# Operands at other places in SBUF, a decay by one product, and VectorE steps in another order, in a decoder layer in split fp32

## The reference

```python
x = x + 0.5 * swiglu_ffn(x, ffn1_norm, ...)          # silu(h @ w_gate) * (h @ w_up)) @ w_down, width 2816
h = rms_norm(x, mix_norm); P = h @ w_in              # split into q,k,v,z,a,b | q,k,v | q
y = concat(gated_deltanet(...), moba_attention(...), memory_attention(...))
x = x + y @ w_out
x = x + 0.5 * swiglu_ffn(x, ffn2_norm, ...)
```

## Time and profile before

| | us |
|---|---|
| median of the runs | 994.51 |
| the profiled execution | 994.35 |
| its span | 992.5 |
| TensorE busy | 987.5 (99%) |
| VectorE busy | 685.7 (69%) |
| GpSimd busy | 509.7 (51%) |
| ScalarE busy | 444.7 (45%) |

### The profile page before, as it was taken

One profiled execution on the slowest core, in us unless ns is written; L12 is line 12 of the kernel. 1 busy time (PEld: TensorE's weight loads), 2 busy tenths in 40 slices (PEclk: granted clock), 3 DMA queues, 4 the chain that ended last, 5 costly groups with the idle time before them and its releaser, 6 DMA issues.

```text
span 992.5 us, 16521 instructions
## 1 busy us (share of the span) xinstructions
PE 987.5 (99%) x6833; PEld 872.2 (88%) x6833; DVE 685.7 (69%) x1092; ACT 444.7 (45%) x655; POOL 509.7 (51%) x297
## 2 busy tenths in 40 slices
PE   9999999999999999999999999999999999999998
PEld 7888999999999988788877888888999999999997
DVE  6894976676666497863547764789986676666745
ACT  8642444344443472534456764634343334433341
POOL 0355775676656433543252301645975666756741
PEclk9999999999999999999999999999999999999999
DMA  8432322332123312321221001322132333123312
GB/s 312 154 130 79 128 86 86 128 128 97 74 86 127 114 57 86 127 86 43 85 87 44 3 2 44 127 85 86 50 122 85 128 128 118 53 86 127 128 43 85
DMA packets 15914, 95.33 MB, mean 96 GB/s; under 512 B 2016, under 2 KB 2400, under 8 KB 5600
## 3 DMA queue, kind: packets, MB, share of 16 engines
q1 hardware_dynamic: 15696, 94.23, 26.4%
q10 hardware_dynamic: 144, 0.05, 0.0%
HBM read 92.17 MB, written 2.10 MB: 95 GB/s over the span
## 4 chain that ended last, share of the span: by engine, by line
PE 96%; DVE 3%; POOL 1%; issue 0%; ACT 0%; DVEq 0%; POOLq 0%
PE bank L2016 50%; PE bank L2142 35%; PE bank L2456 1%; PE bank L2542 1%; PE bank L2460 1%; PE bank L2482 1%; PE bank L2570 1%; PE bank L2559 1%; PE bank L2504 1%; PE bank L2194 1%; POOL wlo L517 0%; PE bank L2526 0%; DVE t_ffn_sum L1339 0%; PE bank L2606 0%; PE bank L2516 0%; PE bank L2628 0%
## 5 line engine op out<-in xcount | busy, mean ns | idle before, releaser
L2142 PE MATMUL bank<-t_ffn_hi,whi 128*128 128x256 f32 x952 | 269.4, 283 | 0.0
L2142 PE MATMUL bank<-t_ffn_hi,wlo 128*128 128x256 f32 x952 | 269.4, 283 | 0.0
L2142 PE MATMUL bank<-t_ffn_lo,whi 128*128 128x256 f32 x952 | 269.4, 283 | 0.0
L534 POOL TENSOR_TENSOR wlo<-sums,whi 128x512 fp32r<-128x512 f32 x136 | 184.7, 1380 | 131.8 <-ACT whi L739 131.7
L517 POOL TENSOR_TENSOR wlo<-raw,whi 128x1024 fp32r<-128x1024 f32 (+1 forms) x36 | 124.6, 3478 | 166.2 <-ACT whi L614 151.3
L534 POOL TENSOR_TENSOR wlo<-raw,whi 128x512 fp32r<-128x512 f32 x102 | 168.4, 1665 | 41.0 <-ACT whi L739 41.0
L2142 PEld LDWEIGHTS bank<-t_ffn_hi,whi 128*128 128x128 f32 x952 | 182.7, 192 | 0.7
L2142 PEld LDWEIGHTS bank<-t_ffn_lo,whi 128*128 128x128 f32 x952 | 182.7, 192 | 0.7
L2142 PEld LDWEIGHTS bank<-t_ffn_hi,wlo 128*128 128x128 f32 x952 | 182.7, 192 | 0.0
L2016 PE MATMUL bank<-ahi,whi 128*128 128x512 f32 x396 | 156.5, 395 | 0.4 <-POOL wlo L517 0.4
L2016 PE MATMUL bank<-ahi,wlo 128*128 128x512 f32 x396 | 154.4, 390 | 0.0
(11 more groups left out here) (339 smaller groups left out, 1405.1 us busy)
## 6 DMA issues: line engine op xcount, KB each, us to landing
raw<-fast_in SPq DMA_DIRECT2D x34, 1024.0 KB, 4.9
raw<-stream SPq DMA_DIRECT2D x26, 1024.0 KB, 4.9
raw_down<-fast_in SPq DMA_DIRECT2D x19, 1024.0 KB, 7.0
raw<-stream SPq DMA_DIRECT2D x7, 512.0 KB, 7.9
out<-x SPq DMA_DIRECT2D x7, 256.0 KB, 2.0
x<-x_in SPq DMA_DIRECT2D x3, 512.0 KB, 8.7
memx<-mem_in SPq DMA_DIRECT2D x2, 512.0 KB, 11.1
raw_gate<-stream SPq DMA_DIRECT2D x1, 1024.0 KB, 5.0
```

The costliest lines, as they stand in the source:

```text
L534: nc.gpsimd.tensor_tensor(in_ring(wlo, ring_at, n), whole[:, PIECE * at:PIECE * (at + 1)], in_ring(whi, ring_at, n).bitcast(F32), ALU.subt ...
L2142: ins = E.matmul(psum[bank][:, HALF * h:HALF * (h + 1)], a, b[:, k, :], start=start and k == 0 and m == 0, stop=k == K2 - 1 and m == 2, sk ...
```

## The change

The code below is the change without lines that only follow from it. It has four parts.

- Places. 64 bytes are left free behind `alo` and again behind `mv`, the x-sum operands get offsets. Worked out modulo 256 from the sizes: raw, whi, wlo, ck, cv, kt and what follows begin at 64; x, ahi, alo, z, mq, cq, the hidden parts stay at 0. The seven operands of the first feed-forward begin at 32. Those of the second begin at 32 (T_B11), 64 (T_1), 192 (T_3), 160 (T_2), 224 (T_B21), 64 (T_B22) and 128 (T_4), which is -96 to +192 bytes from before.
- Decay. `blocks` holds the decay in partitions 64 to 95 and the key factors in 0 to 63, so one tile serves both; `late_decays` makes the rows of chunks 2 and 3 with one product each, into banks 0 and 1.
- Order. On VectorE a MEMSET, evacuate(25), prep_decay(2), level_update(0, 6) and the row maxima of pair 0 move; in the second feed-forward ffn_add 3 moves ahead of a sum of weights. ScalarE and TensorE lists are ordered to match, and chunk 2 changes two banks.
- Head. VectorE makes the high part of x for k = 0. There are 10 warm matmuls instead of 11, on a tile of 128 columns read four times over. For k = 0 to 2 the matmuls are ordered by product.

```diff
@@ places
         alo, a_lo0, _ = place("alo", [P, KD, T], F32R)
+        cursor[0] += 2 * SHIFT
@@
         mv, _, _ = place("mv", [P, NC_, M])
+        cursor[0] += 2 * SHIFT
@@
-        memsq, _, _ = place("memsq", [P, KD, M], at=cq_at)
-        warm, _, _ = place("warm", [P, T], F32R, at=mid)
+        memsq, _, _ = place("memsq", [P, KD, M], at=cq_at + 2 * SHIFT)
+        warm, _, _ = place("warm", [P, P], F32R, at=mid)
@@
-        t_at = [[z_at, z_at + EIGHT, z_at + 2 * EIGHT, a_hi0, a_hi0 + EIGHT, a_lo0, a_lo0 + EIGHT],
-                [a_lo0, a_lo0 + EIGHT, cq_at, kt_at, kt_at + EIGHT, z_at, z_at + EIGHT]]
+        z_t, cq_t, a_hi_t, a_lo_t, kt_t = (at + SHIFT for at in (z_at, cq_at, a_hi0, a_lo0, kt_at - 2 * SHIFT))
+        t_at = [[z_t, z_t + EIGHT, z_t + 2 * EIGHT, a_hi_t, a_hi_t + EIGHT, a_lo_t, a_lo_t + EIGHT],
+                [a_lo_t, a_lo_t + EIGHT + 32, cq_t + 160, kt_t - 128, kt_t + EIGHT - 64, z_t + 32, z_t + EIGHT + 96]]
@@
-        PREP_BANKS = [(4, 5, 6), (4, 5, 6), (0, 4, 6), (1, 5, 0)]
+        PREP_BANKS = [(4, 5, 6), (4, 5, 6), (0, 6, 4), (1, 5, 0)]
@@ ScalarE, head
-                for d in range(PIECES[i], PIECES[i + 1]):
+                for d in range(max(PIECES[i], 1), PIECES[i + 1]):
+                    if d == 1:
+                        act.wait_ge(a_hi, 1)
                     x_high(0, S_G1, d)
@@ ScalarE, middle
             level_copy(0, 6)
+            mem_copy(5)
+            prep_decay(2)
             mem_weights(7, 0)
             mem_weights(7, 1)
-            mem_copy(5)
-            prep_decay(2)
             prep_decay(3)
-            weights(0, 0)
             mem_copy(6)
             prep_keys(2)
+            weights(0, 0)
@@ VectorE, head
+            dve.wait_ge(small_sem, 16)
+            dve.wait_ge(x_sem[0], 16)
+            V.tensor_scalar(x_hi[0][:, 0, :], x[:, 0, :], col(S_G1), None, ALU.mult).then_inc(a_hi, 1)
@@ VectorE, feed-forward
                 ffn_add(before, 2)
+                if f == 1:
+                    ffn_add(before, 3)
                 first_sums(f, 0, 1)
-                ffn_add(before, 3)
+                if f == 0:
+                    ffn_add(before, 3)
@@ VectorE, middle
-            V.memset(xt[half[1], 0:2, :, half[0]], 0.0).then_inc(corner_zero, 1)
             mk_scale(0)
             mq_scale(0)
+            V.memset(xt[half[1], 0:2, :, half[0]], 0.0).then_inc(corner_zero, 1)
@@
             mq_scale(1)
+            evacuate(25, z[:, 3, :])
@@
             mem_scale(5, 1)
-            evacuate(25, z[:, 3, :])
+            prep_decay(2)
@@
             mem_scale(6, 1)
-            prep_decay(2)
             prep_decay(3)
+            level_update(0, 6)
+            mem_out(5)
+            prep(2)
+            prep_scores(2)
             row_max(0, 0)
-            mem_out(5)
             row_max(0, 1)
-            prep(2)
-            level_update(0, 6)
-            prep_scores(2)
             prep_query(2)
@@ TensorE, head
-                for (w, act_), (done, count) in zip(((whi, ahi), (wlo, ahi), (whi, alo)),
-                                                    ((a_hi, 1), (piece_lo, 1), (a_lo, 1))):
-                    pe.wait_ge(done, count)
-                    for bank in range(4):
-                        E.matmul(psum[bank][:], wslice(w, 0, 0, bank * P, P, PAIR), act_[:, 0, :],
-                                 start=w is whi and act_ is ahi, stop=False)
-                for k in range(1, KD):
+                for k in range(3):
+                    low = (piece_lo, k + 1) if k < 2 else (w_lo, 1)
+                    pe.wait_ge(*((piece_hi, k + 1) if k < 2 else (w_hi, 1)))
+                    for (w, act_), (done, count) in zip(((whi, ahi), (wlo, ahi), (whi, alo)),
+                                                        ((a_hi, k + 1), low, (a_lo, k + 1))):
+                        pe.wait_ge(done, count)
+                        for bank in range(4):
+                            E.matmul(psum[bank][:], wslice(w, 0, k, bank * P, P, PAIR), act_[:, k, :],
+                                     start=k == 0 and w is whi and act_ is ahi, stop=False)
+                for k in range(3, KD):
@@
-                    for _ in range(11):
-                        E.matmul(psum[4][:], warm[:, 0:P], warm[:], start=True, stop=True)
+                    for _ in range(10):
+                        E.matmul(heads(4), warm[:], warm[:].unsqueeze(1).broadcast_to([P, H, P]), start=True, stop=True)
@@ TensorE, decay
-            def prep_decay(c):
-                if c == 2:
-                    pe.wait_ge(mk_ready, 5)
-                else:
-                    pe.wait_ge(p_evac, 26)
-                for h in range(H):
-                    i = E.matmul(heads(PREP_BANKS[c][0])[:, h, :], gcol(G_G, h, c).broadcast_to([P, P]), upper,
-                                 start=True, stop=True)
+            def late_decays():
+                pe.wait_ge(mk_ready, 5)
+                E.matmul(psum[PREP_BANKS[2][0]][:], picks[:, 2:3].broadcast_to([P, P]), blocks,
+                         start=True, stop=True).then_inc(w_used, 1)
+                pe.wait_ge(p_evac, 26)
+                E.matmul(psum[PREP_BANKS[3][0]][:], picks[:, 3:4].broadcast_to([P, P]), blocks,
+                         start=True, stop=True).then_inc(prep_ps[0], 2)
@@ TensorE, waits
                 elif c == 2:
-                    pe.wait_ge(y_sb, 3 * LAST)
+                    pe.wait_ge(x_upd, n_x(0, LAST))
@@
-                if c == 3:
+                if c == 2:
+                    pe.wait_ge(y_sb, 3 * LAST)
+                elif c == 3:
@@ TensorE, middle
-            prep_decay(2)
+            late_decays()
             level_first(0, 6)
             mem_scores(7)
             mem_turn(5)
-            prep_decay(3)
             prep(2)
+            level_second(0, 6)
+            mem_out(5)
+            prep_scores(2)
+            mem_turn(6)
+            prep_turn(2)
             scores(0)
-            mem_out(5)
-            level_second(0, 6)
-            mem_turn(6)
-            prep_scores(2)
             mem_out(6)
-            prep_turn(2)
```

More of the change, by code:

```diff
@@ L39 @@
 RING = 3
+SHIFT = 32
 EARLY = 4
@@ L62 @@
 C_BLK = C_SEL + 2
-C_PICK = C_BLK + 8
+C_PICK = C_BLK + 4
 C_N = C_PICK + 12
@@ L123, in build @@
         columns_, columns_at, _ = place("columns", [P, P])
-        column_parts, _, _ = place("column_parts", [P, 2, 16], F32R, at=columns_at)
+        column_parts, _, _ = place("column_parts", [P, 2, 16], F32R, at=columns_at + 64 * 4)
         factor_parts, _, _ = place("factor_parts", [P, 2, 32], F32R, at=columns_at)
@@ L1605, in mk_blocks @@
                 dve.wait_ge(mkbc_ps, 1)
-                spread_blocks(psum[0][:, 0:P], C_BLK + 4).then_inc(mk_ready, 1)
+                spread_blocks(psum[0][:, 0:P], C_BLK).then_inc(mk_ready, 1)
             V.memset(columns_[:], 0.0).then_inc(dve_chain, 1)
@@ L2164, in first_pair @@
             def first_pair():
-                pe.wait_ge(piece_hi, 1)
-                pe.wait_ge(a_hi, 1)
-                for (w, act_), (done, count) in zip(((whi, ahi), (wlo, ahi), (whi, alo)),
-                                                    ((a_hi, 1), (piece_lo, 1), (a_lo, 1))):
-                    pe.wait_ge(done, count)
-                    for bank in range(4):
-                        E.matmul(psum[bank][:], wslice(w, 0, 0, bank * P, P, PAIR), act_[:, 0, :],
-                                 start=w is whi and act_ is ahi, stop=False)
-                for k in range(1, KD):
+                for k in range(3):
[8 more added lines that the diff above has]
+                for k in range(3, KD):
                     pe.wait_ge(a_hi, k + 1)
@@ L2377, in block_decay @@
                          start=True, stop=True).then_inc(prep_ps[0], 1)
-            def prep_decay(c):
-                if c == 2:
-                    pe.wait_ge(mk_ready, 5)
-                else:
-                    pe.wait_ge(p_evac, 26)
-                for h in range(H):
-                    i = E.matmul(heads(PREP_BANKS[c][0])[:, h, :], gcol(G_G, h, c).broadcast_to([P, P]), upper,
-                                 start=True, stop=True)
-                    if c == 2 and h == 0:
-                        i.then_inc(w_used, 1)
-                i.then_inc(prep_ps[0], 1)
+            def late_decays():
[5 more added lines that the diff above has]
+                         start=True, stop=True).then_inc(prep_ps[0], 2)
             def prep(c):
@@ L2880, in constants @@
     r = np.where(i < 64, i % 16, -64)[:, None]
+    decay = np.where((i >= 64) & (i < 96), i % 16, -64)[:, None]
     keys = (i // 16 % 2 == 1)[:, None]
     n = np.arange(4)[None, :]
-    c[:, C_BLK:C_BLK + 4] = r // NC_ == n
-    c[:, C_BLK + 4:C_BLK + 8] = (r >= 0) & (r % 8 // 2 == n)
-    c[:, C_PICK:C_PICK + 4] = (r >= 0) & (r % NC_ == n)
+    c[:, C_BLK:C_BLK + 4] = ((r >= 0) & (r % 8 // 2 == n)) | (decay // NC_ == n)
+    c[:, C_PICK:C_PICK + 4] = (decay >= 0) & (decay % NC_ == n)
```

## The result

The changed kernel takes 1000.89 us (median of four runs, 999.79 to 1001.93) against 994.50 for the kernel before; the ratio is 1.0066, 95% interval 1.0053 to 1.0079. It is 6.4 us slower where 13.4 us less were forecast. The four times fall into two pairs, 999.8 and 1000.0, 1001.8 and 1001.9; the profiled execution took 999.79 for a span of 998.0 and is one of the first pair. It stands 5.4 above the profiled one of before.

The account below looks back on a forecast made before the run. TensorE, busy 987.5 us of a 992.5 us span, was taken as the bound. The terms -8 - 3 - 1.2 - 0.4 - 0.5 - 0.3 = -13.4 us took 994.5 to 981.1, rounded to 981, range 968 to 993.5.

Parts of the forecast that it names:

- The 512-column matmuls, -3: Long matmuls, weights moved 64 bytes: -3 us, between no gain and -6.1; bounds -15 and +18.
- the 264-column rows: Twenty-four matmuls in the earlier trace whose operand start moves by 32 bytes: 120.4 ns each, 10.4 lost beside the columns.
- The x-sum matmuls, -8: 256-column matmuls of the feed-forwards at new places: 2856 x 2.9 ns = -8.3, taken as -8 us; bounds -21 and +24.
- the 2.9: Nanoseconds each x-sum matmul was to save at its new place, by the mean of the 264-column rows.
- Part 2, -1.2: Decay stage: two products replace 8 + 8 matmuls, net -1.4 us, of which 1.2 let through; bounds -1.6 and 0.
- Part 3, the MEMSET, -0.4: VectorE's MEMSET moved behind mq_scale(0), removing TensorE's wait before 525.71 us: -0.4 us; bounds -0.5 and -0.1.
- Part 3, the add, -0.5: Second feed-forward, ffn_add 3 ahead of the sum of weights, removing the wait before 697.67 us: -0.5 us; bounds -0.5 and +0.2.
- Part 4, -0.3: Head: VectorE makes the first x high part, first real matmul at 5.9 to 6.0 us: -0.3 us; bounds -0.6 and +1.4.
- D: Rival: new places meet worse, each x-sum matmul loses 4.2 ns more, +12.0 us, total 1004.1; chance 0.15.
- C: Rival: places change no pace, 13.3 ns is a fixed price of a weight change, total 992.1; chance 0.26.
- The page's rule: TensorE has independent read ports for streamed operand and weights; by it the change of places would be worth nothing.
- the 13.3 ns: What each matmul, short or long, loses beside its columns in the earlier trace: 68 us over 5100 matmuls.

Follow-up runs that it names:

- the map: Computation left out, matmuls alone, weights and streamed operand each at eight offsets in 32-byte steps; at distance 0, 226.7 ns for 512 columns and 120.0 for 256.
- places_undone: The changed kernel with the places alone taken back, decay, order and head kept; 992.44 us, ratio 0.9984 against the kernel before.
- warm_eleven: places_undone with eleven warm matmuls instead of ten; 992.22 us.
- add_back: warm_eleven with the fourth ffn_add of the second feed-forward back behind the sum of weights; 992.28 us.
- deep: The changed kernel with 512-column operands and rings at 0 modulo 256, x-sum operands at distance 112 or -64, eleven warm matmuls; 978.94 us, ratio 0.9850.

## Why the prediction was wrong, step by step

**The 512-column matmuls, -3: the step that failed.** The prediction wrote: "if the distance counts they gain as much each as the others: 2100 x 2.9 = -6.1". The distance counts, and they lose: +5.62 ns x 2271 = +12.8 us, where the sum had -3. The error is in "as the others". The estimate came from the 264-column rows, one short form, and was carried to a form twice as long. The map shows that the two lengths have opposite preferences: at 0 the short one is at its 120.0, near its worst, the long one at its best. The sentence "the all-aligned case is near the bad end" was true for 343 us of TensorE's time and false for 507. The trace of before had a hint: its own long matmuls show 235 just after a change of form and then fall to 226.7. It was used as the upper bound (+18, of which the measured value takes two thirds), but the value was set between the two readings of the 264-column rows, and the range stopped at 993.5, with this bound outside it.

**The x-sum matmuls, -8.** Right in sign, too large: -1.40 ns each, -4.0 us. Half of the 2.9 was due, because 224, where the whole first feed-forward stands, is one of the middling distances (118.2 to 118.7). The reading by distance also foretold that T_1 and T_B22 of the second feed-forward would keep their pace: their means are 119.6 and 119.1, the others of it at 117.9 to 118.9, but T_2 (distance 96, 119.8 to 120.1 in the map) at 119.7.

**Part 2, -1.2.** Right by the traces; no kernel undid it alone. Between places_undone and before the lead of TensorE grows from +0.58 us at the matmul that follows the last pairs product (531.66 against 531.08) to -0.62 at 597.47 against 598.09: 1.20 us. In the changed kernel two products stand for eight and eight matmuls:

```profile
539.08 0.49 PE L2395 MATMUL bank<-blocks,picks 128*128 128x512 f32 x1
539.41 0.40 PE L2398 MATMUL bank<-blocks,picks 128*128 128x512 f32 x1
539.74 0.73 PE L2476 MATMUL bank<-xn,at 64*64 64x64 f32 x9
```

They cost 0.66 us, not 0.55: each takes 0.33 to the next start, where one of them was to take 0.23. The code has a wait ahead of each.

**Part 3, the MEMSET, -0.4.** Right: 0.5, from +1.10 to +0.58 over that stretch of the same two traces. In the changed kernel the matmul that waited 0.25 us has no wait, and the MEMSET stands behind mq_scale(0) (the first row is TensorE, the second VectorE):

```profile
529.70 0.40 PE L2589 MATMUL bank<-blocks,pairs_pick 128*128 128x512 f32 x1
530.99 0.48 DVE L1879 MEMSET xt<- 64x512 f32 x1 [0.16 <-issue]
```

**Part 3, the add, -0.5.** The gain came and was given back. The wait of the earlier trace rows is gone, 0.48 us for the matmul at 697.09 and no idle time before it. But GpSimd's low parts did not move with TensorE, since the sum of weights ahead of them ends when it did: warm_eleven and add_back, which differ in this move alone, have its end at 694.84 and 694.82 us and GpSimd's low part at 712.49 and 712.44. In the changed kernel, 25 us later, TensorE stands in front of them for 0.56 us, where before it had 0.1 (timeline: VectorE's sum, GpSimd, TensorE):

```profile
698.73 2.28 DVE L1364 TENSOR_TENSOR sums<-raw 128x1024 f32<-128x1024 f32 x1
718.65 3.33 POOL L538 TENSOR_TENSOR wlo<-sums,whi 128x512 fp32r<-128x512 f32 x1
722.03 0.39 PE L2154 MATMUL bank<-t_ffn_hi,whi 128*128 128x256 f32 x1 [0.56 <-POOL wlo L538]
```

The prediction saw both ends of this ("-0.5 and +0.2, since TensorE is then 0.5 us earlier at the weights from GpSimd") and took the wrong one; add_back against warm_eleven has them cancel. Where another engine sets the pace of a unit, a wait removed ahead of it comes back there.

**Part 4, -0.3.** The first real matmul starts at 6.06 instead of 6.31 us, the forecast's 5.9 to 6.0 nearly. VectorE's high part takes 0.49 us from 5.42 on (timeline; the earlier trace rows has ScalarE's 0.72):

```profile
5.42 0.49 DVE L1241 TENSOR_SCALAR ahi<-x,small 128x512 fp32r<-128x512 f32 x1 [5.42 <-DMA x<-x_in]
```

Its upper bound, "+1.4 if the clock rises only six matmuls later", is what the profile of places_undone shows, with eight matmuls at the lower level, and probably why two of the four runs of the changed kernel lie 2 us above the others; those have no profile. "One warm matmul less is inside this" left out that TensorE then stands idle before the first real matmul, which goes with the late runs.

**The rivals.** D was on the right side, at 1004.1 with a chance of 0.15, and its mechanism, weight loading and streamed operand hitting each other more often, fits what the map shows; its place was wrong (the x sums, which became faster). It reasoned with half of the 8.4 ns of the earlier trace rows, on 2856 short matmuls; 5.6 ns on 2271 long ones is nearly the same sum, 12.8 against 12.0. C is out: the loss beside the columns is no fixed price, it goes from 6.7 ns (113.3 at 256 columns) to 26.7 (240.0 at 512).

**The page's rule.** The Trainium skill, page "TensorE: Matmul & The Clock Gate", section "Step-by-step: what each phase is for", lets the loading of weights take no read bandwidth from the running matmul. The runs speak against it: with no other engine and no DMA at work, the pace goes with the distance between the two operands, 226.7 to 240.0 ns at 512 columns. That the two reads hinder each other is concluded from this; where they meet, the runs don't show. The prediction's other rule, N/2.4 + 2.5 ns from the section "Back-to-back issue gap", was set against the wrong thing: in the Trainium skill that section gives it for a single matmul by itself, so the 13.3 ns of a stream with a weight load ahead of each matmul are another case.

## What to carry to other kernels

A place in SBUF is a property of a pair, the streamed operand and the weights that load beside it, and its price has to be measured for each number of columns: in these runs an aligned pair was best for 512 columns and nearly worst for 256. Never carry a price in nanoseconds from a short form to a long one; multiply by the count of each form first, and see which form holds the time. When pads are added to shift one set of tiles, list what lies behind them: here 64 bytes ahead of the weight rings changed the distance of some 2100 long matmuls, in a change that was made for the short ones.

## What the runs showed that was not expected

- The pace of back-to-back matmuls is a fixed pattern that repeats (231, 236, 231, 236 ns at distance 192, 240 in a row at 20). At 512 columns its mean is the same to the nanosecond in a kernel with no other load and in the real one.
- At distances 64 and 192 the short form has two patterns, 113.3 and 117.8 ns; which one it falls into depends on what ran before. So a map made in one order need not hold in another: T_B11 of the first feed-forward in deep, at 112, runs at 116.5 to 119.4 where the map has 113.3.
- In the profile of places_undone the granted clock stands at 1.00 while eight matmuls run at the 1.2 GHz level (427 ns for 512 columns); here the distance between starts tells the level, and that column doesn't.
